# Weighing the rows of an expert block on ScalarE and GpSimd instead of VectorE

## The reference

```python
def expert_block(args):
    xblk, e = args
    return (jax.nn.silu(xblk @ w1[e]) * (xblk @ w3[e])) @ w2[e]
...
y = (yb[dest] * wts.reshape(-1)[order][:, None]).astype(xf.dtype)
return jnp.zeros_like(xf).at[tok].add(y)
...
x = x + gx2 * _moe(...)      # gx2: the last modulation row, 1,024 wide
```

## Time and profile before

| what | value |
|---|---|
| time, median of 3 runs | 901.26 us (900.67 to 901.73) |
| the profiled execution: span of its instructions | 899.0 us |
| median time less that span | 2.26 us |
| TensorE busy | 867.7 us (97%) |
| VectorE busy | 637.7 us (71%) |
| ScalarE busy | 409.8 us (46%) |
| GpSimd busy | 186.8 us (21%) |

### The profile page before, as it was taken

The page is one execution under the profiler, slowest core; times in us unless marked ns, Lnnn a source line. Parts: engine busy times, 40 slices in busy tenths (PEclk is TensorE's granted clock), DMA queues, the critical chain, the costliest instruction groups (busy, mean ns, idle before and its releaser), DMA issues.

```text
span 899.0 us, 15366 instructions
## 1 busy us (share of the span) xinstructions
PE 867.7 (97%) x5532; PEld 737.1 (82%) x5533; DVE 637.7 (71%) x907; ACT 409.8 (46%) x574; POOL 186.8 (21%) x225
## 2 busy tenths in 40 slices
PE   8999999999999999999799999999999999999993
PEld 6789878888996667887688888988898888888882
DVE  1678755699767657567885578499846647599995
ACT  3584456111225422222524265476634525477782
POOL 4042001100000010110042233133313222234333
PEclk9999999999999999999979999999999999999997
DMA  9954566511035123123957969799989587599994
GB/s 342 340 176 125 172 194 196 156 47 48 1 141 188 47 95 117 72 94 125 387 198 227 324 183 359 216 333 377 376 258 314 178 243 239 183 342 376 373 365 160
DMA packets 81844, 195.27 MB, mean 217 GB/s; under 512 B 4407, under 2 KB 12812, under 8 KB 81802
## 3 DMA queue, kind: packets, MB, share of 16 engines
q1 hardware_dynamic: 70656, 158.87, 49.7%
q0 software_dynamic: 8272, 25.84, 11.5%
q10 hardware_dynamic: 2874, 10.01, 2.8%
HBM read 169.57 MB, written 25.71 MB: 217 GB/s over the span
## 4 chain that ended last, share of the span: by engine, by line
PE 84%; DVE 11%; issue 2%; POOL 1%; ACT 1%; DMA 1%; ACTq 0%; POOLq 0%; DVEq 0%
PE ps L2386 28%; PE ps L2047 9%; PE ps L2397 9%; PE ps L2050 7%; PE ps L2402 4%; PE ps L2380 2%; PE ps L2247 2%; PE ps L2238 1%; PE ps L2239 1%; PE ps L2240 1%; DVE arena L1380 1%; PE ps L2189 1%; PE ps L2103 1%; PE ps L2021 1%; PE ps L2066 1%
## 5 line engine op out<-in xcount | busy, mean ns | idle before, releaser
L2386 PE MATMUL ps<-w3h,xTh 128*128 128x256 f32 x368 | 105.9, 288 | 0.0
L2386 PE MATMUL ps<-w3h,xTl 128*128 128x256 f32 x368 | 104.1, 283 | 0.0
L2386 PE MATMUL ps<-w3l,xTh 128*128 128x256 f32 x368 | 104.1, 283 | 0.0
L1112 ACT ACTIVATE w1h<-raw 128x2048 fp32r (+1 forms) x32 | 61.1, 1912 | 60.5 <-PE ps L2402 40.3
L1811 DVE TENSOR_TENSOR w1l<-raw,w1h 128x2048 fp32r<-128x2048 f32 x30 | 68.6, 2286 | 26.9 <-ACT w1h L1112 26.9
L2386 PE MATMUL ps<-w2h,hTh 128*128 128x512 f32 x184 | 77.1, 419 | 0.5
L1112 ACT ACTIVATE w2h<-raw 128x2048 fp32r (+1 forms) x32 | 61.3, 1917 | 28.3 <-PE ps L2386 25.2
L1811 DVE TENSOR_TENSOR w3l<-raw,w3h 128x2048 fp32r<-128x2048 f32 x32 | 73.1, 2287 | 0.0
L745 POOL DMA_INDIRECT x_rows<-arena,block_dst x21 | 49.9, 2374 | 109.2 <-DVE arena L1829 109.2
L2397 PE MATMUL ps<-w1h,xTh 128*128 128x512 f32 x184 | 72.4, 393 | 0.0
L2386 PE MATMUL ps<-w2l,hTh 128*128 128x512 f32 x184 | 72.2, 392 | 0.0
(11 more groups left out here) (411 smaller groups left out, 2147.7 us busy)
## 6 DMA issues: line engine op xcount, KB each, us to landing
raw<-in_w_dram SPq DMA_DIRECT2D x48, 2048.0 KB, 12.3
arena<-in_w_mod_dram SPq DMA_DIRECT2D x32, 512.0 KB, 4.0
arena<-in_x_dram SPq DMA_DIRECT2D x16, 512.0 KB, 9.5
arena<-in_w_mod_dram SPq DMA_DIRECT2D x3, 2048.0 KB, 13.9
arena<-in_w_in_dram SPq DMA_DIRECT2D x6, 1024.0 KB, 6.8
x_rows<-arena ACTq DMA_DIRECT2D x9, 512.0 KB, 2.9
hx_rows<-arena ACTq DMA_DIRECT2D x9, 512.0 KB, 4.4
wo_f<-in_w_out_dram SPq DMA_DIRECT2D x2, 2048.0 KB, 8.6
```

What stands on the lines that cost most here:

```text
L1112: act.activation(half_of(j, w_hi[j][:, :], k), half_of(j, raw[:, bass.ds(base, UNIT)], k), ACT.Copy).then_inc(w_high[j], 1)
L2386: ins = pe.matmul(out_ap, parts[l][:, lhs], w_parts[w][:, cols], start=start and n == 0, stop=stop and n == 2)
```

## The change

VectorE's `weigh` leaves the loop. ScalarE gets `scale_rows(b)`: two activations of 128x512 from PSUM with the slot weight as scale, into `ysb[:, 1, :]`. GpSimd gets `gain_rows(b)`: one tensor_tensor of 128x1024 that multiplies `ysb[:, 1, :]` by the modulation row `g2b` into `ysb[:, 0, :]`, ahead of `add_rows(b)`. TensorE waits for the new semaphore `y_scaled` for its banks. Since `early_x` is the same buffer as `ysb[:, 1, :]`, behind the loop the gather into it now follows `gain_rows(before_last)`, and the gather into `last_x` goes first. The last block keeps VectorE's fused form.

```diff
+            def gain_rows(b):
+
+                pool.wait_ge(S["y_scaled"], 2 * b + 4)
+                pool.sem_inc(S["load_seen"], 1)
+                pool.tensor_tensor(ysb[:, 0, :], ysb[:, 1, :], g2b, ALU.mult).then_inc(S["y_ready"], 2)
+                pool.wait_ge(S["y_ready"], 2 * b + 4)
+                pool.sem_inc(S["load_seen"], 1)
...
                         pool.wait_ge(S["y_added"], 16 * b)
-                        pool.sem_inc(S["y_free"], 1)
-                        pool.wait_ge(S["y_ready"], 2 * i + (2 * s + 6))
+                        pool.sem_inc(S["load_seen"], 1)
+                        gain_rows(b)
                         add_rows(b, 1 - s)
...
             pool.wait_ge(S["y_added"], 16 * before_last)
-            pool.sem_inc(S["y_free"], 1)
             pool.sem_inc(S["rows_added"], 1)
             pool.wait_ge(S["dst_ready"], 2)
-            end_gather(0, early_x)
             pool.wait_ge(w_split[1], 2 * NE)
             end_gather(1, last_x)
+            gain_rows(before_last)
+            end_gather(0, early_x)
...
+            def scale_rows(b):
+                act.wait_ge(S["l2_done"], b + 1)
+                act.wait_ge(S["y_ready"], 2 * b + 2)
+                act.sem_inc(S["load_seen"], 1)
+                for h in range(2):
+                    act.activation(ysb[:, 1, h * HALF:(h + 1) * HALF], ps[:, 6 + h, :], ACT.Copy, scale=slot_w[:, bass.ds(b, 1)])\
+                        .then_inc(S["y_scaled"], 1)
...
                     high(2, place[2] * UNIT, 0)
-                    act.wait_ge(S["l2_done"], b + 1)
-                    act.sem_inc(S["load_seen"], 1)
+                    scale_rows(b)
                     high(2, place[2] * UNIT, 1)
...
-            def weigh(b):
-                dve.wait_ge(S["l2_done"], b + 1)
-                dve.wait_ge(S["y_free"], b + 1)
-                for h in range(2):
-                    weigh_half(b, h)
...
-                    weigh(b)
                     low(2, place[2] * UNIT, e + 1, 0)
                     low(2, place[2] * UNIT, e + 1, 1)
...
-                pe.wait_ge(S["y_ready"], y_count)
+                pe.wait_ge(S["y_scaled"], y_count)
```

More of the change, by code:

```diff
@@ L286, in hybrid_block @@
             hTh_a hTh_b hT_a hT_b
-            l2_half l2_done pads_stored y_ready y_added y_free rows_added last_sum
+            l2_half l2_done y_scaled pads_stored y_ready y_added rows_added last_sum
             fout_ready rows_stored""".split()
@@ L787, in _ @@
             next_places(0, 0)
-            pool.wait_ge(S["y_ready"], 4)
+            pool.wait_ge(S["g2_loaded"], 16)
+            gain_rows(0)
             add_rows(0, 0)
@@ L1140, in _ @@
             turn_out(0)
+            act.wait_ge(S["table_ready"], 2)
             def block(b):
@@ L1825, in hidden_low, with weigh_half @@
                     .then_inc(S["hT_b" if k else "hT_a"], 1)
-            def weigh_half(b, h, rows_out=ysb[:, 0, :]):
+            def weigh_half(b, h, rows_out):
                 cols = slice(h * HALF, (h + 1) * HALF)
@@ L1842, in _ @@
             dve.wait_ge(S["rank_done"], 3)
-            dve.tensor_copy(slot_w[:, :], ps[:, 5, 0:NB])
+            dve.tensor_copy(slot_w[:, :], ps[:, 5, 0:NB]).then_inc(S["table_ready"], 1)
             dve.wait_ge(S["g2_loaded"], 16)
@@ L2375, in _ @@
             pe.sem_inc(S["y_ready"], 2)
+            pe.sem_inc(S["y_scaled"], 2)
             def turn_block(b):
```

## The result

| | before | after |
|---|---|---|
| median on one chip, 7 runs each | 901.26 us (900.38 to 905.29) | 907.61 us (906.54 to 909.04) |
| ratio, 95% interval | 1 | 1.0055 [1.0036, 1.0075] |
| span of the profiled execution | 899.0 us | 905.3 us |
| TensorE, VectorE busy | 867.7, 637.7 us | 871.0, 623.3 us |
| ScalarE, GpSimd busy | 409.8, 186.8 us | 434.6, 252.1 us |

The kernel became slower by 6.35 us in the median and 6.3 us in the span; the forecast was 908.4 us. But it was a sum of two terms, 3.1 us in the loop and 4.0 at the end, and the trace shows another split.

The account below looks back on a forecast made before the run. The prediction took TensorE to bound the loop, with VectorE tight at new-expert turns and the end. Span 899.0 + 3.1 (loop) + 4.0 (end) = 906.1 us; with 2.26 from span to median, 908.4 us, range 903.3 to 914.0.

Parts of the forecast that it names:

- What bounds the kernel: Loop: TensorE, busy 18.16 of 18.20 us in a new-expert block; work taken off VectorE gains nothing by itself.
- ScalarE at nothing: Loop: two added activations, 1.3 us per block, cost nothing on the path, covered by TensorE's w1 product.
- GpSimd, how long: GpSimd's 128x1024 multiplication: 2.4 us, the middle between bounds of 1.2 and 3.6 us.
- GpSimd, when: New-expert blocks: multiplication starts when VectorE's first low of w2 ends; VectorE's next low waits until 831.1 instead of 829.6.
- The loop, summed: Turns between new-expert blocks: 3 first turns at 0.2 us and 5 later ones at 0.5 us, 3.1 us in all.
- The end, summed: Behind the loop: the gather into early_x, now after the multiplication, delays VectorE's addition and stops TensorE for 4.0 us.
- A delay of that addition is a delay of the end, one for one: Last block: lateness of VectorE's addition of before_last's product to early_x lengthens the end by the same time.
- only the end: Rival: GpSimd doesn't hold VectorE up, the loop costs nothing, span 905.3 us; chance 0.22, shared with a short multiplication.
- Faster: Rival: TensorE's 15 short loop stops end, gaining 6.5 us against 4.0 lost at the end, 898.8 us; chance 0.06.

Follow-up runs that it names:

- own_short: own_buffer with GpSimd's multiplication cut to 64 of the 1,024 columns; ratio to the kernel before 0.9984.
- own_buffer: Changed kernel, but the early rows of x are gathered into the free buffer xg, ahead of the last multiplication; ratio to before 1.0037.
- late_add: Changed kernel with VectorE's addition into early_x moved behind the last block's hidden halves; ratio to before 1.0029.
- repaired_swap: repaired, with ScalarE making the second hidden half ahead of the copy of the next rows; ratio to before 1.0001.
- end_only: Kernel before with end_moved's order and one unused 128x1,024 GpSimd multiplication ahead of the gather into early_x; ratio to before 1.0055.
- end_moved: Kernel before with only the gather into early_x issued later, as in the changed kernel, and no GpSimd multiplication; ratio to before 1.0008.
- busy13: Changed kernel with 13 unused matmuls of ones on TensorE ahead of its wait for the last block's hidden half; ratio to before 1.0042.
- before_swap: Kernel before with ScalarE making the second hidden half ahead of the copy of the next rows; ratio to before 0.9987.
- scale_late: Changed kernel with ScalarE's two scalings moved behind the second high half of w2; ratio to before 1.0049.
- repaired: own_buffer, scale_late and late_add together on the changed kernel; ratio to before 1.0010.

## Why the prediction was right, and where it was wrong

The time, the sign and the range held. Of the steps:

- *What bounds the kernel*: right. Work taken off VectorE gave nothing, the loop's turns stayed as they were, the end carried the loss.
- *ScalarE at nothing*: right for the turns up to block 22, as own_short shows, whose 364.25 us have the scalings in them. The two take 1.27 us. The turn before the last block may be longer by them, through weights that land later; that is not shown.
- *GpSimd, how long*, 2.4 us: 2.27 measured once the port is free.
- *GpSimd, when*: right, including the direction that no row showed. The Trainium skill, page "SBUF — State Buffer", section "Who interferes with whom", was right that the holding goes both ways: up to 2.6 us more in a low of VectorE (4.91 in own_buffer against 2.28).
- *The loop, summed*, 3.1 us: **wrong**, -0.2 in after by the count from block 2 to 22 (up to 2.0 in late_add, and then by late weights). The failed step is the sentence "VectorE's block is 17.3 - 1.4 + 2.4 + the 0.64 that it waits for ScalarE". The 0.64 is a wait, and a wait shrinks when the waiter comes later: it fell to 0.30. The 2.4 stood for the delay of the second low, which is a new wait of 1.19 and 0.96 of holding, 2.15. 17.3 - 1.4 + 2.15 + 0.30 gives 18.3, TensorE's own turn. (The 17.3 is 17.21 in the earlier trace rows.) I had added up busy time and a wait of the old schedule as if both were fixed. repaired_swap shows such a term once TensorE's turn would be 18.0: 0.57 us a turn, in a kernel with the scalings moved.
- *The end, summed*, 4.0 us: the addition moved by 3.68. The chain named did end last, but **the reason given covers only 0.38 of it**. In the chain the multiplication ended at 869.0, not 867.7, and the gather landed in 6.3 us, not 7.9, which brought 876.1 near the 876.5 forecast. By the distance from the last block's start it is 3.14 later (11.42 against 8.28): 1.55 because VectorE reaches L1893 later (6.62 us into the block, 5.07 before), 1.06 of waiting for the roots behind the multiplication, 0.38 for the gather, 0.15 in small pieces. Of the 1.55 the longer exit is 1.35. The holding alone gave 2.2 us in end_only, which has the short exit; in after it ran beside the exit. end_moved shows the gather's place alone at 0.2 us, and end_only the multiplication with it at 6.0. The forecast followed one dependence, the gather's, and not the others that queue behind the same GpSimd instruction.
- *"A delay of that addition is a delay of the end, one for one"*: **wrong by 2.5 us**. The stop of 2.98 us also cost TensorE its upper clock. The forecast had 4 us of idle TensorE in it and no word on what follows one; busy13 and late_add keep the clock up, and the end is shorter by it.
- The errors were 3.3 us too much in the loop, 1.8 too little at the end, and no term for the 0.8 of the turn before the last block. They cancelled to 0.8 us of span, 906.1 against 905.3. That the median was hit this closely is luck.
- *Rivals*: "only the end" was the right case in its place, with another price (5.8 us, not 4.0). "Faster" named the short stops and doubted that VectorE's weighing made them: rightly, they came from ScalarE's order (before_swap).

## What to carry to other kernels

Before a step goes to an idle engine, list everything that stands behind it there, and what its port shuts out; one multiplication of 2.3 us on a GpSimd that was 21% busy cost 6 us in end_only, and the 21 of them in the loop of after cost nothing that its trace shows. Add up a cycle with its waits as results, not as terms: each shrinks as its engine comes later. And price a stop of TensorE with what its clock does behind it.

## What the runs showed of the hardware that I had not expected

- TensorE's granted clock after a stop. After stops of 0.2 to 1.4 us the two transposes lay 3.1 us apart. After 2.45, 2.98, 3.09, 4.18 and 4.39 us they lay 4.61, 5.61, 5.61, 4.39 and 4.34 apart, with stretches at 0.50 of full clock. The longest stops didn't cost most: in scale_late, whose stop ended at 878.3, the clock was back at 1.00 from 882 on, as its stretches show (columns as above):

```profile
878.00:880.00 2.00, 1.67 (x8) 1.68 (x9) 1.41 (x4) 0.95 (x2) 0.00 (x0) 0.50 0.04 16
880.00:882.00 2.00, 2.00 (x12) 1.87 (x11) 1.01 (x3) 1.62 (x3) 0.74 (x2) 0.71 0.04 8
882.00:884.00 2.00, 2.00 (x11) 1.64 (x10) 1.59 (x3) 0.91 (x2) 0.00 (x0) 1.00 0.04 14
```

- VectorE's exit from the loop: 1.79 us idle before its first instruction behind it in own_short, scale_late and repaired, whose `block` on VectorE lacks the weighing, and 1.35 in repaired_swap, which lacks it too, against 0.45 to 0.47 in before, end_moved and before_swap, which have it. The wait for ScalarE is not its cause (scale_late). What is, stays open; padding the loop to its old length wasn't tried.
- A row's duration includes the time in which the other engine held the port, on VectorE (2.28 grew to as much as 4.91 us) as on GpSimd (2.3 to 2.4 grew to 2.9 to 4.25).
